# Differential-attention core of a hybrid trunk: both score rows reduced and awaited in one step, squares of the head outputs on GpSimd a tile at a time, one more item in flight

## The chip, the cores and the metric

The kernel runs on one core of one Trainium2 chip. The metric is the device time of one execution in microseconds (us). The core has TensorE (PE, with its weight loads PEld), the Vector engine (DVE), the Scalar engine (ACT), GpSimd (POOL) and the DMA queues issued by SyncE (SP). Matrix products land in PSUM, here eight banks of 512 float32 per partition; everything else lies in SBUF.

## The reference, cut to what matters

The trunk has two layers: a convolution and state-space mixer with a dense SwiGLU, then differential attention with a mixture of experts. The change is inside the attention of the second layer: 512 tokens, 8 pairs of heads, head size 64, values of 128 per pair.

```
q, k = apply_rope(rmsnorm(q, q_norm)), apply_rope(rmsnorm(k, k_norm))
lam = exp(sum(lam_q1*lam_k1)) - exp(sum(lam_q2*lam_k2)) + lambda_init
for q0 in range(0, s, 128):                       # 4 query blocks
    sc = q[q0:q0+128] @ k[:q0+128].T / sqrt(64)   # 16 heads = 8 pairs x 2
    p  = softmax(where(kpos//64 <= qpos//64, sc, -inf))
    a  = p[first of pair] - lam * p[second of pair]
    o  = a @ v[:q0+128]                           # 128 x 128 for each pair
o = rmsnorm(o, sub_norm) * (1 - lambda_init)      # mean square over the 128 of a pair
out = o @ w_o
```

## The kernel before, in words

Everything is float32. The attention core (lines 702 to 735 on TensorE, 952 to 984 on the Scalar engine, 1395 to 1428 on the Vector engine) works through 32 items. An item is one query tile `i` of 128 tokens and one pair; `items` (line 702) goes through the tiles from last to first, so items 0 to 7 see w = 512 keys, 8 to 15 see 384, 16 to 23 see 256, and 24 to 31 see 128. Each engine runs the same Python loop over `n` with its own program order; semaphores tie them together. The word "step n" below means iteration n of that loop.

In step n of the kernel before:

- TensorE computes the two score rows of item n (line 713, with the 64-column mask as a second small product, line 715) into banks 0 and 1 or 2 and 3, turns the difference of item n-2 (line 724, four 128x128 transposes at w = 512) into bank 4 or 5, and multiplies the turned difference of item n-3 with v (line 733) into bank 6 or 7, in this order.
- The Vector engine takes the maximum of each score row of item n in an instruction of its own (line 1402), drains, multiplies both by -SCALE (line 1404, `bias_ready`), then for item n-1 takes the reciprocals of the two softmax sums (line 1412), forms -lambda * sum0 / sum1 (line 1414) and the difference `probs0 + s * probs1` (line 1418), and last scales the output of item n-3 from PSUM into `o_tok` (line 1423, `heads_evac`).
- The Scalar engine takes the two exponentials of item n with their sums (line 962), with a drain and a semaphore after each (line 964), copies the turned difference of item n-2 to SBUF (line 971, `diffT_ready`), and squares the output of item n-3 with a sum into `head_ss` (line 976). In step 31 it takes the square root over the sums of the first three tiles (line 980).
- GpSimd does nothing in the core. In the rest of the layer it makes the low parts `w_lo` of the weights (line 1022); its next one follows the core.

`probs`, `diff`, `diffT` and the score banks have two buffers each, `soft` (maxima, sums, factors) four. After the loop the Vector engine scales the four tiles of `o_tok` by the reciprocal roots (`heads_norm`, lines 1381 to 1393), and TensorE turns them and begins the output projection (line 524). The Vector engine's program order in a step is thus maxima(n), difference(n-1), output(n-3).

Of the kernel before, what the change touches and what calls it, by code (L numbers as in the profile page):

```python
# [16 lines left out]
F32 = mybir.dt.float32  # L17
# [7 lines left out]
P = 128  # L25
# [16 lines left out]
NEG = -1e30  # L42
# [54 lines left out]
def build_trunk(nc, t, y_dram, h_slots):  # L97
# [74 lines left out]
    probs, o = place("probs", [P, 2, 2, SEQ], F32, scratch)  # L172
    diff, o = place("diff", [P, 2, SEQ], F32, o)
    diffT, o = place("diffT", [P, 2, SEQ], F32, o)
    soft, _ = place("soft", [P, 4, 8], F32, scratch + 65536)
# [17 lines left out]
    def sem(name):  # L193
# [31 lines left out]
    diff_turned, diffT_ready, heads_out, heads_evac = (sem("diff_turned"), sem("diffT_ready"),  # L225
                                                       sem("heads_out"), sem("heads_evac"))
# [138 lines left out]
    def _(pe):  # L365
# [338 lines left out]
        for n in range(N + 3):  # L704
            if n < N:
                pair, i = items[n]
                w = P * (i + 1)
                if n >= 2:
                    pe.wait_ge(exp_done, 2 * (n - 1))
                for m in range(2):  # L710
                    r = slice(64 * m, 64 * m + 64)
                    b = 2 * (n % 2) + m
                    pe.matmul(ps[:, b, 0:w], qT[r, pair, i * P:(i + 1) * P], kT[r, pair, 0:w],
                              start=True, stop=False, skip_group_check=True)
                    mm = pe.matmul(ps[:, b, w - 64:w], att_small[r, 0:P], att_small[r, P:P + 64],
                                   start=False, stop=True, skip_group_check=True)
                mm.then_inc(scores_done, 1)
            if 2 <= n < N + 2:
                pair, i = items[n - 2]
                pe.wait_ge(diff_ready, n - 1)  # L720
                if n >= 4:
                    pe.wait_ge(diffT_ready, n - 3)
                for b in range(i + 1):
                    mm = pe.transpose(ps[:, 4 + n % 2, b * P:(b + 1) * P],
                                      diff[:, n % 2, b * P:(b + 1) * P], ident[:])
                mm.then_inc(diff_turned, 1)
            if n >= 3:
                pair, i = items[n - 3]
                pe.wait_ge(diffT_ready, n - 2)
                if n >= 5:  # L730
                    pe.wait_ge(heads_evac, n - 4)
                for b in range(i + 1):
                    mm = pe.matmul(ps[:, 6 + (n - 3) % 2, 0:P], diffT[:, (n - 3) % 2, b * P:(b + 1) * P],
# [14 lines left out]
    def _(act):  # L748
# [205 lines left out]
        for n in range(N + 3):  # L954
            if n < N:
# [3 lines left out]
                if n >= 2:  # L959
                    act.wait_ge(diff_ready, n - 1)  # L960
                for m in range(2):
                    act.activation(probs[:, n % 2, m, 0:w], ps[:, 2 * (n % 2) + m, 0:w], ACT.Exp, scale=SCALE,
                                   bias=soft[:, n % 4, m:m + 1], accum_out=soft[:, n % 4, 2 + m:3 + m])
                    act.drain().then_inc(exp_done, 1)
            if 2 <= n < N + 2:
                pair, i = items[n - 2]
                w = P * (i + 1)
                act.wait_ge(diff_turned, n - 1)
                if n >= 4:
                    act.wait_ge(heads_out, n - 3)  # L970
                act.activation(diffT[:, n % 2, 0:w], ps[:, 4 + n % 2, 0:w], ACT.Copy).then_inc(diffT_ready, 1)
            if n >= 3:
                pair, i = items[n - 3]
                act.wait_ge(heads_evac, n - 2)
# [4 lines left out]

# [34 lines left out]
    def _(pool):  # L1014
# [70 lines left out]
        for half in range(2):  # L1085
# [7 lines left out]
            low_parts(u0 + FF_HALF - 1 + AHEAD)  # L1093
        low_parts(N_UNITS - 1)
# [3 lines left out]
    def _(dve):  # L1098
# [220 lines left out]
        dve.wait_ge(att_in, 128)  # L1319
        for i in range(2):  # L1320
# [21 lines left out]
        for r in (0, 64):  # L1342
            dve.memset(att_small[r:r + 1, 0:64], NEG)
# [51 lines left out]
        for n in range(N + 3):  # L1395
            if n < N:
                pair, i = items[n]
                w = P * (i + 1)
                s2 = soft[:, n % 4, :]
                dve.wait_ge(scores_done, n + 1)  # L1400
                for m in range(2):
                    dve.reduce_max(s2[:, 6 + m:7 + m], ps[:, 2 * (n % 2) + m, 0:w], AX.X)
                dve.drain()
                dve.tensor_scalar(s2[:, 0:2], s2[:, 6:8], -SCALE, None, ALU.mult).then_inc(bias_ready, 1)
            if 1 <= n <= N:

                pair, i = items[n - 1]
                w = P * (i + 1)
                b = (n - 1) % 2
                s2 = soft[:, (n - 1) % 4, :]  # L1410
                dve.wait_ge(exp_done, 2 * n)
                dve.reciprocal(s2[:, 4:6], s2[:, 2:4])
                dve.drain()
                dve.tensor_scalar(s2[:, 5:6], s2[:, 5:6], s2[:, 2:3], stat[:, 61:62], ALU.mult, ALU.mult)
                if n >= 3:
                    dve.wait_ge(diff_turned, n - 2)
                dve.drain()
                dve.scalar_tensor_tensor(diff[:, b, 0:w], probs[:, b, 1, 0:w], s2[:, 5:6], probs[:, b, 0, 0:w],
                                         ALU.mult, ALU.add).then_inc(diff_ready, 1)
            if n >= 3:  # L1420
                pair, i = items[n - 3]
                dve.wait_ge(heads_out, n - 2)
                dve.tensor_scalar(o_tok[:, i, pair * P:(pair + 1) * P], ps[:, 6 + (n - 3) % 2, 0:P],
                                  soft[:, (n - 3) % 4, 4:5], None, ALU.mult).then_inc(heads_evac, 1)
            if n > N:
                heads_norm(n - N - 1)
        heads_norm(NT - 2)
# [914 lines left out]
```

## Time and profile before

| | |
|---|---|
| time, median of 3 runs (lowest, highest) | 2041.79 us (2039.48, 2042.93) |
| time of the profiled execution | 2043.4 us |
| span of the profiled execution | 2041.6 us |
| PE busy | 1971.8 us (97%) |
| DVE busy | 749.8 us (37%) |
| ACT busy | 652.1 us (32%) |
| POOL busy | 490.9 us (24%) |
| mean granted TensorE clock | 0.983 |

The span runs from the first instruction to the last; the execution's own time lies 1.8 us above it. The shares are means over stages with different limits. The attention core runs from the first score product at 920.2 us to the first product of the output projection at 1011.9 us, 4.5% of the span.

### The profile page before, as it was taken

The numbers are of one execution on the slowest core, as the hardware profiler recorded it, in microseconds if no ns is written. First come the engines' busy times: TensorE is split into PE (matmuls) and PEld (weight loads), VectorE is DVE, ScalarE is ACT, GpSimd is POOL, SyncE is SP. The second block draws the span as 40 slices with busy tenths as digits, with TensorE's granted clock in tenths as the row PEclk, the third lists the DMA queues.
The fourth block names the chain that finished last, engine by engine and source line by source line (L and its number), as shares of the span: only waits on it lengthen the run. The fifth ranks groups of instructions, "written<-read, shape, count | busy, mean of one in ns | idle before, by whom it ended". The sixth has DMA issues, their size and how long they took to land.

```text
span 2041.6 us, 28889 instructions
## 1 busy us (share of the span) xinstructions
PE 1971.8 (97%) x11899; PEld 1731.5 (85%) x11899; DVE 749.8 (37%) x1138; ACT 652.1 (32%) x1061; POOL 490.9 (24%) x246
## 2 busy tenths in 40 slices
PE   7999999999999999998899999999999999999996
PEld 6787778888888888886688999999999999888885
DVE  4625564210010005948722000010010101989896
ACT  4333223232222224337630000000000011878784
POOL 3446664265445544540011000000000000000010
PEclk9999999999999999999898999999999999999998
DMA  7862222243233232330007977888888898999995
GB/s 241 298 197 74 63 73 93 73 124 93 92 95 103 88 105 75 101 104 1 22 1 268 322 241 260 300 299 302 276 305 288 284 312 278 377 372 374 361 396 212
DMA packets 295087, 405.38 MB, mean 199 GB/s; under 512 B 11264, under 2 KB 211018, under 8 KB 294954
## 3 DMA queue, kind: packets, MB, share of 16 engines
q1 hardware_dynamic: 292650, 395.11, 57.4%
q0 software_dynamic: 2304, 8.39, 1.1%
q8 instruction: 96, 1.57, 0.3%
q14 instruction: 37, 0.30, 0.0%
HBM read 372.67 MB, written 30.80 MB: 198 GB/s over the span
## 4 chain that ended last, share of the span: by engine, by line
PE 88%; DVE 3%; ACT 2%; DVEq 2%; POOL 2%; issue 1%; DMA 1%; SPq 0%; POOLq 0%; ACTq 0%
PE ps L1729 20%; PE ps L1736 10%; PE ps L375 5%; PE ps L376 5%; PE ps L377 5%; PE ps L393 5%; PE ps L394 5%; PE ps L395 5%; PE ps L1787 4%; PE ps L1789 4%; PE ps L1788 4%; PE ps L410 2%; PE ps L412 2%; PE ps L411 2%; DVEq L1186 1%
## 5 line engine op out<-in xcount | busy, mean ns | idle before, releaser
L1022 POOL TENSOR_TENSOR w_lo<-raw,w_hi 128x1024 fp32r<-128x1024 f32 (+1 forms) x159 | 390.3, 2463 | 462.7 <-ACT w_hi L758 462.7
L1563 DVE TENSOR_TENSOR s_lo<-s_raw,s_hi 128x1024 fp32r<-128x1024 f32 x198 | 236.9, 1222 | 28.1 <-ACT s_hi L1933 22.6
L2183 DVE TENSOR_TENSOR hid<-ps,silu_g 128x160 f32<-128x160 f32 x110 | 35.7, 324 | 550.1 <-ACT silu_g L1908 550.1
L1729 PE MATMUL ps<-xT,w_gate 128*128 128x132 f32 (+1 forms) x1760 | 226.6, 282 | 4.6 <-issue 4.0
L758 ACT ACTIVATE w_hi<-raw 128x1024 fp32r<-128x1024 f32 (+1 forms) x159 | 164.8, 1043 | 205.1 <-PE ps L395 136.4
L375 PE MATMUL ps<-act_a_hi,w_hi 128*128 128x512 f32 x568 | 226.3, 398 | 0.0
L1729 PE MATMUL ps<-xT,w_up 128*128 128x132 f32 (+1 forms) x1760 | 224.4, 281 | 0.0
L1908 ACT ACTIVATE silu_g<-ps 128x160 f32<-128x160 f32 x110 | 33.5, 304 | 593.3 <-PE ps L1729 593.3
L1933 ACT ACTIVATE s_hi<-s_raw 128x1024 fp32r<-128x1024 f32 x198 | 206.7, 1061 | 51.0 <-PE ps L1789 46.5
L377 PE MATMUL ps<-act_a_hi,w_lo 128*128 128x512 f32 x568 | 221.2, 389 | 0.0
L376 PE MATMUL ps<-act_a_lo,w_hi 128*128 128x512 f32 x568 | 221.1, 389 | 0.0
L1729 PEld LDWEIGHTS ps<-xT,w_gate 128*128 128x128 f32 x1760 | 216.2, 191 | 5.1 <-issue 4.2
L1736 PE MATMUL ps<-hid,w_down 128*128 128x132 f32 (+1 forms) x1760 | 214.8, 281 | 0.0
L1729 PEld LDWEIGHTS ps<-xT,w_up 128*128 128x128 f32 x1760 | 214.6, 190 | 0.0
L1736 PEld LDWEIGHTS ps<-hid,w_down 128*128 128x128 f32 x1760 | 209.8, 190 | 0.2
L2028 POOL DMA_INDIRECT y_lower<-y_rows,idx x4 | 5.3, 1334 | 825.8 <-DMA y_rows<-y_rows_sb 824.8
L375 PEld LDWEIGHTS ps<-act_a_hi,w_hi 128*128 128x128 f32 x568 | 106.7, 188 | 27.1 <-issue 5.3
L376 PEld LDWEIGHTS ps<-act_a_lo,w_hi 128*128 128x128 f32 x568 | 106.7, 188 | 24.6 <-issue 2.9
L377 PEld LDWEIGHTS ps<-act_a_hi,w_lo 128*128 128x128 f32 x568 | 106.6, 188 | 22.3
L1787 PE MATMUL ps<-s_hi,s_x_hi 128*128 128x512 f32 (+1 forms) x288 | 109.8, 381 | 0.0
L1789 PE MATMUL ps<-s_hi,s_x_lo 128*128 128x512 f32 (+1 forms) x288 | 107.9, 375 | 0.0
L1788 PE MATMUL ps<-s_lo,s_x_hi 128*128 128x512 f32 (+1 forms) x288 | 107.0, 372 | 0.0
(355 smaller groups left out, 2949.1 us busy)
## 6 DMA issues: line engine op xcount, KB each, us to landing
w_gate<-in_moe_w_gate SPq DMA_DIRECT2D x55, 1024.0 KB, 5.6
w_up<-in_moe_w_up SPq DMA_DIRECT2D x55, 1024.0 KB, 8.5
w_down<-in_moe_w_down SPq DMA_DIRECT2D x55, 1024.0 KB, 11.0
s_raw<-in_moe_w_gate SPq DMA_DIRECT2D x33, 1024.0 KB, 7.6
s_raw<-in_moe_w_up SPq DMA_DIRECT2D x33, 1024.0 KB, 8.3
s_raw<-in_moe_w_down SPq DMA_DIRECT2D x33, 1024.0 KB, 7.7
raw<-in_even_w_in SPq DMA_DIRECT2D x43, 512.0 KB, 4.5
raw<-in_attn_w_qkv SPq DMA_DIRECT2D x24, 512.0 KB, 3.8
```

The lines of the kernel that those rows point to most:

```text
L375: pe.matmul(ps[:, bank, :], wh, xh[:, k, :], start=(k == 0), stop=False)
L376: pe.matmul(ps[:, bank, :], wh, xl[:, k, :], start=False, stop=False)
L377: last = pe.matmul(ps[:, bank, :], wl, xh[:, k, :], start=False, stop=(k == KD - 1))
L758: act.activation(w_hi[:, u % HL_SLOTS, 0:size(u)], raw[:, u % RAW_SLOTS, 0:size(u)], ACT.Copy).then_inc(hi_done, 1)
L1022: pool.tensor_tensor(w_lo[:, u % HL_SLOTS, 0:size(u)], raw[:, u % RAW_SLOTS, 0:size(u)], flat(w_hi[:, u % HL_SLOTS, 0:size(u)]), ALU.subtr ...
L1563: return eng.tensor_tensor(s_lo[u % S_HL][:], s_raw[u // 2 % S_RAW][:, u % 2, :], s_hi[u % S_HL][:].bitcast(F32), ALU.subtract)
L1729: mm = pe.matmul(ps[:, bank, i * CAP:i * CAP + width], w_slots[s][i][:, k, c:c + P], xT[:, k, 0:width], start=(k == 0), stop=(k == KD - 1))
L1736: mm = pe.matmul(ps[:, d // 3, (d % 3) * CAP:(d % 3) * CAP + width], w_slots[s][2][:, f % 2, d * P:(d + 1) * P], hid[:, f, 0:width], start ...
L1787: pe.matmul(out, sh, wh, start=first, stop=False, skip_group_check=True)
L1788: pe.matmul(out, sh, wl, start=False, stop=False, skip_group_check=True)
L1789: return pe.matmul(out, sl, wh, start=False, stop=last, skip_group_check=True)
L1933: act.activation(s_hi[u % S_HL][:], s_raw[q % S_RAW][:, u % 2, :], ACT.Copy).then_inc(s_high, 1)
```

## The change

The gain of the q norm is multiplied by -SCALE once, before the loop, so that the scores in PSUM are already the negated scaled ones; the mask adds +1e30. One `tensor_reduce` with min over both banks gives the two biases directly. The exponential uses scale -1, and one drain and one semaphore follow both. `probs` gets a third buffer, `soft` eight. Transposes run on item n-3 and head products on item n-4. The Vector engine's order in a step becomes minima(n), output(n-4), difference(n-1), and the factor is made by one `scalar_tensor_tensor`. The squares of the first three tiles are taken on GpSimd, each tile in two instructions of 128x512 once its eight outputs are in `o_tok`, and summed on the Vector engine by a reduction of 128x1024 at the end of steps 15, 23 and 31; the Scalar engine squares only the last tile's items. The Scalar engine's root in step 31 waits for the three sums.

```diff
--- before.py
+++ after.py
@@ -39,7 +39,7 @@
-NEG = -1e30
+MASKED = 1e30
@@ -169,10 +169,10 @@
     sq_tmp, o = place("sq_tmp", [P, SEQ], F32, o)
     qT, o = place("qT", [P, KD, SEQ], F32, SEQ * NT * 4 * 2)
     kT, o = place("kT", [P, KD, SEQ], F32, o)
-    probs, o = place("probs", [P, 2, 2, SEQ], F32, scratch)
+    probs, o = place("probs", [P, 3, 2, SEQ], F32, scratch)
     diff, o = place("diff", [P, 2, SEQ], F32, o)
-    diffT, o = place("diffT", [P, 2, SEQ], F32, o)
-    soft, _ = place("soft", [P, 4, 8], F32, scratch + 65536)
+    diffT, o = place("diffT", [P, 2, SEQ], F32, scratch + 3 * NT * D * 4)
+    soft, _ = place("soft", [P, 8, 8], F32, scratch + 65536)
     o_tok, o = place("o_tok", [P, NT, D], F32, scratch + NT * D * 4)
 
     h_tok, _ = place("h_tok", [P, NT, D], F32, NT * D * 4)
...
@@ -701,12 +702,12 @@
 
         items = [(pair, i) for i in reversed(range(NT)) for pair in range(PAIRS)]
         N = len(items)
-        for n in range(N + 3):
+        for n in range(N + 4):
             if n < N:
                 pair, i = items[n]
                 w = P * (i + 1)
                 if n >= 2:
-                    pe.wait_ge(exp_done, 2 * (n - 1))
+                    pe.wait_ge(exp_done, n - 1)
                 for m in range(2):
                     r = slice(64 * m, 64 * m + 64)
                     b = 2 * (n % 2) + m
@@ -715,22 +716,22 @@
                     mm = pe.matmul(ps[:, b, w - 64:w], att_small[r, 0:P], att_small[r, P:P + 64],
                                    start=False, stop=True, skip_group_check=True)
                 mm.then_inc(scores_done, 1)
-            if 2 <= n < N + 2:
-                pair, i = items[n - 2]
-                pe.wait_ge(diff_ready, n - 1)
-                if n >= 4:
-                    pe.wait_ge(diffT_ready, n - 3)
+            if 3 <= n < N + 3:
+                pair, i = items[n - 3]
+                pe.wait_ge(diff_ready, n - 2)
+                if n >= 5:
+                    pe.wait_ge(diffT_ready[(n - 5) % 2], (n - 5) // 2 + 1)
                 for b in range(i + 1):
-                    mm = pe.transpose(ps[:, 4 + n % 2, b * P:(b + 1) * P],
-                                      diff[:, n % 2, b * P:(b + 1) * P], ident[:])
+                    mm = pe.transpose(ps[:, 4 + (n - 3) % 2, b * P:(b + 1) * P],
+                                      diff[:, (n - 3) % 2, b * P:(b + 1) * P], ident[:])
                 mm.then_inc(diff_turned, 1)
-            if n >= 3:
-                pair, i = items[n - 3]
-                pe.wait_ge(diffT_ready, n - 2)
-                if n >= 5:
-                    pe.wait_ge(heads_evac, n - 4)
+            if n >= 4:
+                pair, i = items[n - 4]
+                pe.wait_ge(diffT_ready[(n - 4) % 2], (n - 4) // 2 + 1)
+                if n >= 6:
+                    pe.wait_ge(heads_evac, n - 5)
                 for b in range(i + 1):
-                    mm = pe.matmul(ps[:, 6 + (n - 3) % 2, 0:P], diffT[:, (n - 3) % 2, b * P:(b + 1) * P],
+                    mm = pe.matmul(ps[:, 6 + (n - 4) % 2, 0:P], diffT[:, (n - 4) % 2, b * P:(b + 1) * P],
                                    v_tok[:, b, pair * P:(pair + 1) * P], start=(b == 0), stop=(b == i))
                 mm.then_inc(heads_out, 1)
         first_tokens(4, U_WO, heads_tile, act_b_hi, act_b_lo)
@@ -951,32 +952,33 @@
             act.activation((qT, kT)[n // 8][:, n % 8, :], ps[:, n % 4, :], ACT.Copy).then_inc(qk_evac[0], 1)
         items = [(pair, i) for i in reversed(range(NT)) for pair in range(PAIRS)]
         N = len(items)
-        for n in range(N + 3):
+        for n in range(N + 5):
             if n < N:
                 pair, i = items[n]
                 w = P * (i + 1)
                 act.wait_ge(bias_ready, n + 1)
-                if n >= 2:
-                    act.wait_ge(diff_ready, n - 1)
+                if n >= 3:
+                    act.wait_ge(diff_ready, n - 2)
                 for m in range(2):
-                    act.activation(probs[:, n % 2, m, 0:w], ps[:, 2 * (n % 2) + m, 0:w], ACT.Exp, scale=SCALE,
-                                   bias=soft[:, n % 4, m:m + 1], accum_out=soft[:, n % 4, 2 + m:3 + m])
-                    act.drain().then_inc(exp_done, 1)
-            if 2 <= n < N + 2:
-                pair, i = items[n - 2]
+                    act.activation(probs[:, n % 3, m, 0:w], ps[:, 2 * (n % 2) + m, 0:w], ACT.Exp, scale=-1.0,
+                                   bias=soft[:, n % 8, m:m + 1], accum_out=soft[:, n % 8, 2 + m:3 + m])
+                act.drain().then_inc(exp_done, 1)
+            if 3 <= n < N + 3:
+                pair, i = items[n - 3]
                 w = P * (i + 1)
-                act.wait_ge(diff_turned, n - 1)
-                if n >= 4:
-                    act.wait_ge(heads_out, n - 3)
-                act.activation(diffT[:, n % 2, 0:w], ps[:, 4 + n % 2, 0:w], ACT.Copy).then_inc(diffT_ready, 1)
-            if n >= 3:
-                pair, i = items[n - 3]
-                act.wait_ge(heads_evac, n - 2)
+                b = (n - 3) % 2
+                act.wait_ge(diff_turned, n - 2)
+                if n >= 5:
+                    act.wait_ge(heads_out, n - 4)
+                act.activation(diffT[:, b, 0:w], ps[:, 4 + b, 0:w], ACT.Copy).then_inc(diffT_ready[b], 1)
+            if n >= N - PAIRS + 5:
+                pair, i = items[n - 5]
+                act.wait_ge(heads_evac, n - 4)
                 act.drain()
                 act.activation(sq_tmp[:, 0:P], o_tok[:, i, pair * P:(pair + 1) * P], ACT.Square,
                                accum_out=head_ss[:, 8 * i + pair:8 * i + pair + 1])
             if n == N - 1:
-
+                act.wait_ge(o_sum, NT - 1)
                 act.activation(head_ss[:, 40:64], head_ss[:, 8:32], ACT.Sqrt, scale=1.0 / P,
                                bias=stat[:, 60:61]).then_inc(o_rms, 1)
         act.drain()
@@ -1091,6 +1093,22 @@
                 pool.tensor_tensor(ff_lo[:, f, :], ff_val[:, n % 2, :], flat(ff_hi[:, f, :]),
                                    ALU.subtract).then_inc(ff_lo_done, 1)
             low_parts(u0 + FF_HALF - 1 + AHEAD)
+        low_parts(U_WO + AHEAD - 1)
+
+        items = [(pair, i) for i in reversed(range(NT)) for pair in range(PAIRS)]
+        N = len(items)
+
+        def square_half(k, h):
+            tt, c = NT - 1 - k, slice(512 * h, 512 * h + 512)
+            pool.wait_ge(heads_evac, PAIRS * (k + 1))
+            pool.tensor_tensor(htmp[:, c], o_tok[:, tt, c], o_tok[:, tt, c], ALU.mult).then_inc(o_sq, 1)
+
+        for n in range(N):
+            k, at = (n - 12) // PAIRS, (n - 12) % PAIRS
+            if 0 <= k < NT - 1 and at < 2:
+                if at == 0 and k:
+                    pool.wait_ge(o_sum, k)
+                square_half(k, at)
         low_parts(N_UNITS - 1)
 
 
@@ -1317,6 +1335,9 @@
                 add_to_x(G_DOWN[0] + 1, u0 + FF_HALF - 1, 512)
         add_and_norm(2, G_DOWN[1] + 1, U_QKV - 1)
         dve.wait_ge(att_in, 128)
+
+        dve.tensor_scalar(att_small[:, 0:HD], att_small[:, 0:HD], -SCALE, None, ALU.mult)
+        dve.drain()
         for i in range(2):
             g1, g2 = att_small[:, HD * i:HD * i + 32], att_small[:, HD * i + 32:HD * i + 64]
             b1, b2 = (g.unsqueeze(1).to_broadcast([P, NT, 32]) for g in (g1, g2))
@@ -1340,7 +1361,7 @@
-            dve.memset(att_small[r:r + 1, 0:64], NEG)
+            dve.memset(att_small[r:r + 1, 0:64], MASKED)
@@ -1392,39 +1413,40 @@
             if j >= 2:
                 turned_low(4, j - 2, act_b_hi, act_b_lo, small[:, 63:64])
 
-        for n in range(N + 3):
+        for n in range(N + 4):
             if n < N:
                 pair, i = items[n]
                 w = P * (i + 1)
-                s2 = soft[:, n % 4, :]
                 dve.wait_ge(scores_done, n + 1)
-                for m in range(2):
-                    dve.reduce_max(s2[:, 6 + m:7 + m], ps[:, 2 * (n % 2) + m, 0:w], AX.X)
-                dve.drain()
-                dve.tensor_scalar(s2[:, 0:2], s2[:, 6:8], -SCALE, None, ALU.mult).then_inc(bias_ready, 1)
+                dve.tensor_reduce(soft[:, n % 8, 0:2], ps[:, 2 * (n % 2):2 * (n % 2) + 2, 0:w], AX.X, ALU.min
+                                  ).then_inc(bias_ready, 1)
+            if n >= 4:
+                pair, i = items[n - 4]
+                dve.wait_ge(heads_out, n - 3)
+                dve.tensor_scalar(o_tok[:, i, pair * P:(pair + 1) * P], ps[:, 6 + (n - 4) % 2, 0:P],
+                                  soft[:, (n - 4) % 8, 4:5], None, ALU.mult).then_inc(heads_evac, 1)
             if 1 <= n <= N:
 
-                pair, i = items[n - 1]
-                w = P * (i + 1)
-                b = (n - 1) % 2
-                s2 = soft[:, (n - 1) % 4, :]
-                dve.wait_ge(exp_done, 2 * n)
+                s2 = soft[:, (n - 1) % 8, :]
+                dve.wait_ge(exp_done, n)
                 dve.reciprocal(s2[:, 4:6], s2[:, 2:4])
                 dve.drain()
-                dve.tensor_scalar(s2[:, 5:6], s2[:, 5:6], s2[:, 2:3], stat[:, 61:62], ALU.mult, ALU.mult)
+                dve.scalar_tensor_tensor(s2[:, 6:7], s2[:, 5:6], stat[:, 61:62], s2[:, 2:3], ALU.mult, ALU.mult)
                 if n >= 3:
                     dve.wait_ge(diff_turned, n - 2)
                 dve.drain()
-                dve.scalar_tensor_tensor(diff[:, b, 0:w], probs[:, b, 1, 0:w], s2[:, 5:6], probs[:, b, 0, 0:w],
-                                         ALU.mult, ALU.add).then_inc(diff_ready, 1)
-            if n >= 3:
-                pair, i = items[n - 3]
-                dve.wait_ge(heads_out, n - 2)
-                dve.tensor_scalar(o_tok[:, i, pair * P:(pair + 1) * P], ps[:, 6 + (n - 3) % 2, 0:P],
-                                  soft[:, (n - 3) % 4, 4:5], None, ALU.mult).then_inc(heads_evac, 1)
+                pair, i = items[n - 1]
+                w = P * (i + 1)
+                dve.scalar_tensor_tensor(diff[:, (n - 1) % 2, 0:w], probs[:, (n - 1) % 3, 1, 0:w], s2[:, 6:7],
+                                         probs[:, (n - 1) % 3, 0, 0:w], ALU.mult, ALU.add).then_inc(diff_ready, 1)
+            if n in (15, 23, 31):
+                k = n // PAIRS - 1
+                i = NT - 1 - k
+                dve.wait_ge(o_sq, 2 * (k + 1))
+                dve.reduce_sum(head_ss[:, 8 * i:8 * i + 8], htmp[:].rearrange("p (h d) -> p h d", h=8), AX.X
+                               ).then_inc(o_sum, 1)
             if n > N:
                 heads_norm(n - N - 1)
-        heads_norm(NT - 2)
         heads_norm(NT - 1)
         for j in (NT - 2, NT - 1):
             turned_low(4, j, act_b_hi, act_b_lo, small[:, 63:64])
```

## Rows read from the trace of the kernel before

**Rows 1.** Stretch, length, busy PE PEld DVE ACT POOL, clock, DMA, GB/s
```profile
920.00:1003.00 83.00, 70.39 (x490) 50.88 (x490) 68.86 (x222) 63.01 (x214) 0.00 (x0) 0.95 0.01 1
```

**Rows 2.** Chain of waits, one cycle at 512 keys: start us, us, what
```profile
936.18 0.69 DVE soft L1402
936.87 0.60 DVEq L1403
937.75 0.69 ACT probs L962
938.62 0.69 ACT probs L962
939.56 0.61 ACT diffT L971
940.21 1.16 PE ps L733 x8
...
942.66 0.69 DVE soft L1402
```

**Rows 3.** Groups by form, 920 to 1012 us: busy us, mean ns, idle
```profile
L1402 DVE TENSOR_REDUCE soft<-ps 128x1 f32<-128x512 f32 x16 | 10.3, 684 | 3.0 <-PE ps L715 3.0
...
L1418 DVE SCALAR_TENSOR_TENSOR diff<-probs,soft 128x512 f32<-128x512 f32 x8 | 6.0, 752 | 0.6
...
L1418 DVE SCALAR_TENSOR_TENSOR diff<-probs,soft 128x128 f32<-128x128 f32 x8 | 2.8, 352 | 0.6
```

**Rows 4.** Timeline, Vector engine, one item at 512 keys: start us, us
```profile
934.13 0.16 DVE L1412 RECIPROCAL soft<-soft 128x2 f32<-128x2 f32 x1
...
934.72 0.75 DVE L1418 SCALAR_TENSOR_TENSOR diff<-probs,soft 128x512 f32<-128x512 f32 x1
...
935.39 0.34 DVE L1423 TENSOR_SCALAR o_tok<-ps,soft 128x128 f32<-128x128 f32 x1
```

**Rows 5.** Timeline, one item at 128 keys, Scalar engine, TensorE
```profile
995.41 0.19 ACT L976 ACTIVATION_READ_ACCUMULATOR sq_tmp<-o_tok 128x1 f32 x1
...
995.50 0.35 ACT L962 ACTIVATE probs<-ps,soft 128x128 f32<-128x128 f32 x1
...
996.66 0.28 ACT L971 ACTIVATE diffT<-ps 128x128 f32<-128x128 f32 x1 [0.16 <-PE ps L724]
...
996.99 0.49 PE L733 MATMUL ps<-v_tok,diffT 128*128 128x128 f32 x2 [0.48 <-ACT diffT L971]
```

**Rows 6.** GpSimd, Vector: by line (ns min/median/max), timeline, by form (mean ns)
```profile
L1366 DVE TENSOR_TENSOR q_tok<-rot_sum,head_ss x8: 691/2613/2619, 808.8 to 844.3; 128x512 f32<-128x512 f32 x8
...
811.66 2.93 POOL L1022 TENSOR_TENSOR w_lo<-raw,w_hi 128x1024 fp32r<-128x1024 f32 x1 [3.93 <-ACT w_hi L758]
...
L1091 POOL TENSOR_TENSOR ff_lo<-ff_val,ff_hi x22: 1289/1295/1301, 431.3 to 716.3; 128x512 fp32r<-128x512 f32 x22
...
293.83 4.26 DVE L1235 TENSOR_TENSOR mix<-mix,cbm 128x512 f32<-128x512 f32 x2
...
L1196 DVE SCALAR_TENSOR_TENSOR dts<-dts 128x64 f32<-128x64 f32 x1 | 0.5, 527 | 0.1
```

**Rows 7.** Chain of waits, from the first exponential to the output projection
```profile
923.12 0.69 ACT probs L962
...
1001.49 0.37 ACT probs L962
...
1003.43 1.28 ACT L980
...
1006.73 1.22 DVE o_tok L1390
1007.95 0.26 DVE o_tok L1423
...
1011.86 0.50 PE ps L524
```

**Rows 8.** As rows 1, for 927 to 929 us
```profile
927.00:929.00 2.00, 2.00 (x6) 0.86 (x6) 1.76 (x5) 1.12 (x3) 0.00 (x0) 0.50 0.04 8
```

More of the change, by code:

```diff
@@ L224, in build_trunk @@
                                                      sem("exp_done"), sem("diff_ready"))
-    diff_turned, diffT_ready, heads_out, heads_evac = (sem("diff_turned"), sem("diffT_ready"),
-                                                       sem("heads_out"), sem("heads_evac"))
+    diff_turned, heads_out, heads_evac = sem("diff_turned"), sem("heads_out"), sem("heads_evac")
+    diffT_ready = (sem("diffT_even"), sem("diffT_odd"))
+    o_sq, o_sum = sem("o_sq"), sem("o_sum")
     o_rms = sem("o_rms")
```

## The prediction, written before the changed kernel was run

> **What bounds the kernel now.** The page first: TensorE is busy for 97% of the span, but that is the mean over long matmul stages that the change does not touch. So I read the stretch of the attention core by itself. There TensorE is busy 70.4 us of 83, the Vector engine 68.9 and the Scalar engine 63.0, GpSimd not at all [rows 1]. No engine is full; a loop of waits through all three should be looked for, and the chain of waits shows it [rows 2]. Its seven pieces repeat: the maxima (0.69 and 0.60), a small step that makes the biases (the exponential starts 1.57 us after the first maximum), two exponentials (0.88 us apart, 1.81 to the copy), the copy of a turned difference (0.65 to the next start), then the head product (1.16) and the scores of the next item but one (2.45 from 940.21 to the next maximum at 942.66). That is 6.48 us for two items, 3.24 for one. Each engine fills some 3.0 of these 3.24. The loop takes two items because the copy stands behind the exponential in the Scalar engine's order and the scores behind the head product in TensorE's. The core gets shorter only if this loop does, or if its replacement is shorter.
>
> **The bias and the exponentials.** One reduction of 1024 elements replaces two of 512. By the slope of the difference (752 - 352) / 384 = 1.04 ns an element, it takes 0.684 + 512 x 0.00104 = 1.22 us [rows 3]; the small step and a drain go. The exponential starts 1.25 us after the reduction instead of 1.57: 0.32 gained. Bounds: if a reduction over two banks costs as two, 1.37, gain 0.17. The drain between the exponentials goes. An accumulator read that no drain follows lets the next exponential start 0.09 us after its own start [rows 5]; the second exponential now starts 0.88 - 0.68 = 0.20 us earlier. Bounds 0 and 0.20; I take 0.20, as the row is the same pair of operations. The old loop would be 6.48 - 0.32 - 0.20 = 5.96, and TensorE's own order (head product 1.16, scores, transposes) needs about 3.00 an item, so 6.0 would be the floor for two.
>
> **The order on the Vector engine, a new loop.** The output copy now stands ahead of the difference. Output(n-4) waits for the head product of TensorE's step n, and behind it on the Vector engine are queued the reciprocals, the factor, difference(n-1) and the reduction of item n+1, whose exponential in turn stands ahead of the copy that the head product of step n+2 needs. This closes a loop of two steps: head product 1.16 and 0.06 to be seen; output copy 0.26 to the next start [rows 7]; reciprocal to difference 0.59, difference to the next start 0.67 [rows 4]; reduction to exponential 1.25; exponential to copy 1.81 - 0.20 = 1.61; copy to product 0.65 [rows 2]. Sum 6.25 us, 3.13 an item. At 128 keys: product 0.49, seen 0.06, output 0.26, factor 0.59, difference 0.27, reduction 0.15 + 0.27 + 0.03 = 0.45, exponential to copy 1.16 - 0.20 = 0.96, rounded to 0.95, copy to product 0.33: 3.40, 1.70 an item [rows 3 to 5]. The one-element factor I take at its old cost; a tenth less or more is 0.1 in each double step. The pieces grow evenly with width between those ends. In the loop before, the output copy came last and this path was shorter than the loop of rows 2, since the reduction did not wait for it through the difference.
>
> **The squares.** Taking them off the Scalar engine gives it back about 0.48 us an item, but it is not in either loop behind the copy; I count nothing for it, and what hides it is that the Scalar engine waits for the bias anyway. What comes in their place is counted: six GpSimd instructions of 128x512, 1.30 us each [rows 6], and three reductions of 128x1024 on the Vector engine, 1.22 less an overlap of 0.07 = 1.15 each. The reductions at steps 15 and 23 stand between a difference and the next reduction, inside the new loop: 2.3 us. The one at step 31 counts in the tail.
> GpSimd starts its first half when the eighth output of a tile is written, so at steps 11, 19 and 27, and just then the Vector engine issues factor and difference. Vector instructions with both inputs in SBUF take 0.69 us alone and 2.61 in most cases while the low parts run on GpSimd [rows 6]; an instruction of 64 elements took 0.53. Where several GpSimd instructions stood in a row, two Vector ones took 4.26 together [rows 6]. So the factor (two SBUF inputs now) waits for the first half, and the difference, issued after a drain, for the second. Without it the difference starts 0.26 + 0.59 = 0.85 us after the output copy; with it 0.43 + 2 x 1.30 = 3.0. That is 2.1 us for each tile, 6.3 for three. Bounds: nothing if the pairs never meet, which the semaphore at that very place makes unlikely, and 2.6 x 3 = 7.8. I take 6.3. Loops without slack pass such a delay on whole; all five disturbances (at 11, 15, 19, 23, 27) fall on the same one of the two interleaved loops, so they add up to 8.6.
> The Trainium skill ("SBUF — State Buffer", section "Who interferes with whom") says that a Vector instruction with two SBUF inputs and a GpSimd instruction that reads SBUF exclude each other for the whole instruction, the one that starts first winning, whatever the shapes. By that rule the one-element factor is held as well, and the sum is 6.3; if a small operand passed freely, only the difference would be held, by the first half, and it would be 3 x 1.0. The 0.53 us of a 64-element instruction [rows 6] speaks for the rule; one of a single element is not in the trace.
>
> **Fill and tail.** The first exponential starts 0.32 us earlier than 923.12 [rows 7]. During the first four items no head product exists that anything waits for, so the items come by scores, reduction and exponential alone, also without the halved clock that TensorE had after its early wait [rows 8]. I follow them with the same pieces: exponentials 0, 2, 4, 6 at 922.8, 926.9, 931.9, 938.8. From there twelve double steps to item 30 (6.0 at first, as widths mix, 3.40 at the end) sum to 56.3: 995.1, and item 31 at 996.8. Before, it was at 1001.49 [rows 7]. So without the disturbances the loop gains 4.6; with the 8.6 it is 4.0 late.
> In the tail the projection came 10.37 us after exponential 31 (1011.86 - 1001.49). Now the Scalar engine's root waits for the third sum, which stands behind difference(30): about 2.7 us after exponential 31; the table load of 1.28 and the root follow, then the copy of item 29, its product, and three more outputs, with norms of 1.22 between them [rows 7]: I get 11.5, a loss of 1.1 us.
> The q gain's multiplication adds a small instruction where the Vector engine waits for the first squares of q: nothing, or 0.3 if that cover were gone. Memory moves and the extra buffers cost no instruction.
>
> **Sum.** -4.6 + 8.6 + 1.1 = +5.1 us. The execution profiled took 2043.4 (span 2041.6), so 2048.5; against the median of the runs, which lies 1.6 lower, 2041.8 + 5.1 = 2046.9. What can be told from no change is 0.2%, 4.1 us, that is 2037.7 to 2045.9.
>
> **Rivals.**
> A, the forecast: new loop, and both factor and difference held. +5.1, 2046.9. For it: the orders, and rows 6. Against: it needs the timing at step 11 to be as written. 0.38.
> B, the same but held only once a tile (a one-element factor passes, or starts first): 3 x 1.1 less, +1.8, 2043.6. 0.27.
> C, the new loop does not bind: head products come early enough, through the extra item in flight, and the floor is TensorE's 3.00 (at 128 keys 2.88 for two). The mean saving is 0.38 in each of twelve double steps, 4.6; holds once a tile, and slack takes 0.3 from each of five disturbances, 1.5: +1.8 - 4.6 - 1.5 = -4.3, 2037.5, faster. For it: the Vector engine has 0.3 us to spare an item. Against: the loop is only 0.25 us above the floor at 512 keys but 0.5 at 128, and I see nothing that would cut it. 0.18.
> D, the clock: TensorE was granted 0.50 at 927 to 929 us [rows 8], after it had waited for the first exponential. Five delays of 1 to 2 us, each a wait of TensorE, might bring this back each time; a product of 1.16 then takes 2.3 and the loop grows by some 1.5 us for such a stretch. Two or three of them: +3.5 on top of A, 2050.4, slower. 0.17.
>
> **How the numbers follow.** A's own spread (bounds 0.17 against 0.32 for the reduction, the factor) is about 2.5 us to either side; six tenths of it lie above 2045.9, the rest within. Slower: 0.23 + 0.17 = 0.40, with a little of B 0.42. Same: 0.15 + 0.25 = 0.39 with the near end of C. Faster: C, 0.19. The range takes C's near end and D's: 2037.5 to 2050.5.
>
> **What would show it.** The reduction of 128x2x512 near 1.22 us, the bias step gone; the second exponential 0.68 us after the first at 512 keys. In the chain, output copy, factor and difference between head product and reduction (if instead scores lead to the reduction throughout, C). One factor or difference of over 1 us at items 7, 15 and 23, the factor of one element among them (B, if only one instruction is long). The sums at 1.2 us with the reduction of the next item right behind. The table load later after exponential 31 than the 1.94 us of before. The clock in windows behind steps 11 and 19. I am wrong if the core, 920.2 to 1011.9 before, is shorter than 88 us or longer than 101.

## The result, and the profile after

| | before | after |
|---|---|---|
| time, median of 13 runs (lowest, highest) | 2041.76 us (2038.36, 2044.44) | 2046.79 us (2044.24, 2047.59) |
| ratio to before, 95% interval | | 1.0021 [1.0014, 1.0029] |
| span of the profiled execution | 2041.6 us | 2044.7 us |
| core: first score product to first product of the output projection | 91.65 us | 95.32 us |

The change makes the kernel slower, by 5.0 us in the medians (4.3 by the ratio, its interval 2.9 to 5.9) and by 3.7 us in the core of the two profiled executions. From here on "core" is that stretch. It is read from one trace of each kernel, and it is sharper than the medians, because the 1950 us around it vary by a few microseconds (1946.2 to 1954.0 us over ten traces here). No trace was repeated for one kernel, so the core's own scatter is not known; experiment 5 shows 0.3 us that its edit does not explain.

The new loop stands in the changed kernel's chain of waits at 512 keys (start us, us, what). Lines 734, 1426, 1440, 1421, 963 and 973 are 733, 1423, 1418, 1402, 962 and 971 of before. The first head product is released by a copy of the Scalar engine, the last closes the loop; pieces of up to 0.22 us are left out:

```profile
930.99 1.17 PE ps L734 x8
932.18 0.35 DVE o_tok L1426
932.98 0.75 DVE diff L1440
933.73 1.15 DVE soft L1421
934.90 0.69 ACT probs L963
935.67 0.67 ACT probs L963 x2
936.50 0.61 ACT diffT L973
937.15 1.16 PE ps L734 x8
```

In [rows 2] the maximum followed the scores; here it follows the output copy and the difference. The cycle is 937.15 - 930.99 = 6.16 us where it was 6.48. The parts that should become cheaper did. In the groups by form (mean ns behind the busy time) the minimum over 2x512 takes 1220 ns against two of 684 in [rows 3]:

```profile
L1421 DVE TENSOR_REDUCE soft<-ps 128x2 f32<-128x1024 f32 x8 | 9.7, 1220 | 1.7 <-PE ps L716 1.6
...
L1446 DVE TENSOR_REDUCE head_ss<-htmp 128x8 f32<-128x1024 f32 x3 | 3.6, 1213 | 0.0
```

On the Scalar engine's timeline (start us, us) the two exponentials of an item start 0.67 us apart, 0.87 before [rows 2]:

```profile
922.00 0.69 ACT L963 ACTIVATE probs<-ps,soft 128x512 f32<-128x512 f32 x1 [3.23 <-DVE soft L1421]
...
922.67 0.68 ACT L963 ACTIVATE probs<-ps,soft 128x512 f32<-128x512 f32 x1
```

What eats the gain is at steps 11, 19 and 27. The timeline of the Vector engine and GpSimd at step 11 (start us, us, engine, line, operation):

```profile
952.58 0.35 DVE L1426 TENSOR_SCALAR o_tok<-ps,soft 128x128 f32<-128x128 f32 x1
...
953.01 2.04 POOL L1104 TENSOR_TENSOR htmp<-o_tok 128x512 f32<-128x512 f32 x2 [43.38 <-DVE o_tok L1426]
...
953.08 0.99 DVE L1434 SCALAR_TENSOR_TENSOR soft<-soft,stat 128x1 f32<-128x1 f32 x1
...
954.14 1.32 DVE L1440 SCALAR_TENSOR_TENSOR diff<-probs,soft 128x384 f32<-128x384 f32 x1
...
955.38 0.95 DVE L1421 TENSOR_REDUCE soft<-ps 128x2 f32<-128x768 f32 x1
```

The squares start 0.07 us ahead of the one-element factor here, and within 0.01 us of it at steps 19 and 27. The factor takes 0.99 us instead of 0.22 and the difference 1.32 instead of 0.62, the one held by the first half, the other by the second. From output copy to next minimum it is 955.38 - 952.58 = 2.80 us, and 1.32 in the step before (950.19 to 951.51): a hold of 1.48, and in the same way 1.54 at each of steps 19 and 27, 4.6 together. Behind the second hold TensorE's granted clock falls to its lower level, 0.50, from about 979 to 986 us (stretch, length, busy us of PE, PEld, DVE, ACT, POOL, granted clock):

```profile
920.00:1003.00 83.00, 67.73 (x482) 51.38 (x478) 64.72 (x149) 48.28 (x154) 6.11 (x6) 0.92 0.00 1
978.00:982.00 4.00, 2.25 (x10) 1.70 (x11) 2.64 (x9) 2.81 (x10) 0.00 (x0) 0.69 0.00 0
982.00:986.00 4.00, 4.00 (x22) 3.30 (x21) 2.57 (x7) 1.40 (x5) 0.00 (x0) 0.50 0.01 2
```

Over the same 83 us as [rows 1] TensorE is busy for 67.7 us instead of 70.4, at 0.92 instead of 0.95. The Scalar engine, freed of 24 squares, is busy for 48.3 instead of 63.0; experiments 2 and 7 show that this time is worth nothing here.

### The profile page after: what moved, and what is told of

It is laid out like the page before. It is cut to its first block, busy times and chain, and to the rows that moved or that the text cites. A ratio compares the mean times of both kernels' runs of the same rounds, so it can differ in the third digit from the quotient of the medians.

```text
span 2044.7 us, 28701 instructions
## 1 busy us (share of the span) xinstructions
PE 1969.6 (96%) x11899; PEld 1732.3 (85%) x11899; DVE 750.5 (37%) x1078; ACT 639.7 (31%) x1013; POOL 497.6 (24%) x252
## 4 chain that ended last, share of the span: by engine, by line
PE 88%; DVE 4%; ACT 2%; POOL 2%; DVEq 2%; issue 1%; DMA 1%; POOLq 0%; SPq 0%; ACTq 0%
PE ps L1751 20%; PE ps L1758 10%; PE ps L376 5%; PE ps L377 5%; PE ps L378 5%; PE ps L394 5%; PE ps L396 5%; PE ps L395 5%; PE ps L1809 4%; PE ps L1811 4%; PE ps L1810 4%; PE ps L411 2%; PE ps L412 2%; PE ps L413 2%; DVEq L1204 1%
```

## Experiments

In each, "exponential k" is the time from exponential 0 to exponential k in the trace. Before: 31 at 78.37; after: 12 at 34.36, 20 at 56.40, 24 at 67.64, 31 at 81.88.

**1. Output copy back behind the difference** (the moved lines in words).

```diff
-            if n >= 4:  (output copy of item n-4, between minima and factor)
+            if n >= 4:  (the same lines, behind the difference of item n-1)
```

> The changed kernel with the output copy put back behind the difference in the Vector engine's step. 'Core' is the time from the first score product to the first product of the output projection: 91.7 us before, 95.3 after. Theory (the output copy ahead of the difference closes a loop of 6.2 us for two items): the core loses some 4.6 us of loop, the holds by GpSimd shrink from 1.5 to about 0.8 us since the squares now start beside the reduction, and the stretch at half clock goes: core 87 to 89 us, time 6 to 8 us under the changed kernel. Rival (the extra item in flight has made the order harmless, only the holds count): core 93 us or more, time at most 2 us less.

Core 86.41 us, time 2037.26, ratio 0.9971 [0.9961, 0.9982] to before. The core is 0.6 us better than my bound, and the medians differ from the changed kernel by 9.5 us where I had 6 to 8. The chain at 512 keys, from head product to head product, is that of before with the cheaper parts, 937.46 - 931.49 = 5.97 us (5.96 forecast as the old loop):

```profile
931.49 1.16 PE ps L734 x8
932.65 1.07 PE ps L714 x4
933.72 0.20 PE ps L716 x4
...
933.94 1.24 DVE soft L1421
...
935.20 0.69 ACT probs L963
...
936.81 0.61 ACT diffT L973
...
937.46 1.16 PE ps L734 x8
```

This run alone mixes the loop with smaller holds: the longest factor is 0.95 us, and of the three differences behind the squares only the last is still held (1.05 us). The next ones part them.

**2. Squares back on the Scalar engine, order kept.**

```diff
-            if n >= N - PAIRS + 5:
+            if n >= 5:
-                act.wait_ge(o_sum, NT - 1)
-   (GpSimd's squares and the Vector engine's sums)
```

> The changed kernel with the squares of every item on the Scalar engine as before, no GpSimd work and no sums in the core, everything else kept. Theory: this takes away the holds (3 x 1.47), two sums inside the loop (2 x 1.13) and the stretch at half clock (about 1.6): core 87 to 89 us against 95.3, and the Scalar engine, which gets 0.48 us an item back to do, is the bound at 128 keys only and by less than 0.1 an item. Rival (the Scalar engine was what the squares had to leave): core 93 us or more.

Core 86.93 us, just under my 87 to 89, time 2038.37, ratio 0.9977 [0.9967, 0.9987]. Exponential 31 at 73.50: the rest of the change, new order and all, gains 4.9 us in the loop. The move to GpSimd costs 8.4 of core. The rival falls: the Scalar engine had room.

**3. Squares a little later.**

```diff
             pool.wait_ge(heads_evac, PAIRS * (k + 1))
+            pool.wait_ge(diff_ready, PAIRS * k + 11 + h)
```

> The changed kernel with each GpSimd half also waiting for a difference to be done (first half for that of its own step, second half for that of the next step), so that neither factor nor difference meets it. Theory: the three holds of 1.47 go and with them part of the half clock: core 89.5 to 91.5 us, time 4 to 6 us under the changed kernel, all factors 0.22 us. Rival (other waits cover the holds): core within 1 us of 95.3.

Core 89.44, time 2040.78, ratio 0.9988 [0.9979, 0.9997]. The longest factor is 0.46 us, so not all are at the 0.22 I had expected; no difference is held. Exponential 12 is at 32.89 (1.47 earlier than in the changed kernel), 20 at 53.41 (2.99), 24 at 62.82 (4.82), 31 at 76.00 (5.88). So the holds are 1.5 us each and pass on whole, and between 20 and 24, where nothing is held and both kernels take one sum, another 1.8 goes. What differs there in the two traces is the clock: 0.50 from 980 to 984 us in the changed kernel, and 1.00 throughout in this run, where these exponentials are at 975.15 and 984.56. I put the 1.8 down to it; no run changes the clock alone.

**4. Is it a busy GpSimd or one that reads SBUF?** Memsets of like length at the same place; the squares of three tiles are left out.

```diff
-            pool.tensor_tensor(htmp[:, c], o_tok[:, tt, c], o_tok[:, tt, c], ALU.mult).then_inc(o_sq, 1)
+            first half:  pool.memset(htmp[:], 1.0).then_inc(o_sq, 1)
+            second half: pool.memset(rot_tmp[:], 1.0); pool.memset(rot_sum[:], 1.0).then_inc(o_sq, 1)
```

> The changed kernel with the GpSimd squares replaced by memsets of about the same length (one of 1024, then two of 512 elements), at the same place and behind the same waits; the squares of three tiles are left out. Theory (the holds come from both engines reading SBUF): factor and difference at 0.22 and 0.35 to 0.62 us throughout, core 89 to 91 us. Rival (a busy GpSimd, or its semaphores, holds the Vector engine): factors of about 1 us at steps 11, 19 and 27, core 94 us or more. The core alone is read, since the routing behind it works on other numbers.

Core 89.50 (time 2399.6 in its one run, not compared: behind the core it works on other numbers), exponentials 12, 20, 24 and 31 at 32.89, 53.39, 62.79 and 76.06: the kernel of experiment 3 within 0.06 us. Timeline of GpSimd at step 11 (start us, us):

```profile
952.80 0.95 POOL L1108 MEMSET htmp<- 128x1024 f32 x1 [43.35 <-DVE o_tok L1430]
953.69 0.52 POOL L1105 MEMSET rot_tmp<- 128x512 f32 x1
954.16 0.52 POOL L1106 MEMSET rot_sum<- 128x512 f32 x1
```

And all 32 factors, by line (ns min/median/max):

```profile
L1438 DVE SCALAR_TENSOR_TENSOR soft<-soft,stat x32: 219/220/221, 923.6 to 1000.7; 128x1 f32<-128x1 f32 x32
```

GpSimd is busy for nearly as long as with the squares (1.9 us against 2.04) and no factor takes more than 221 ns; the longest difference is 0.75 us, as without a hold. A memset writes SBUF and reads nothing, so it is the reading that holds the Vector engine. The Trainium skill ("SBUF — State Buffer", section "Who interferes with whom") has the same: a Vector instruction takes its second SBUF input through the read interface that it shares with GpSimd, so it contends with a GpSimd instruction that reads SBUF and not with one that only writes. The traces agree, and in the changed kernel one element was enough, 0.99 for 0.22 us.

**5. Cheap sums.** The sums take the first column of each head alone; the rest is left out.

```diff
-   htmp[:].rearrange("p (h d) -> p h d", h=8), AX.X
+   htmp[:].rearrange("p (h d) -> p h d", h=8)[:, :, 0:1], AX.X
```

> The changed kernel with its three sums cut to the first column of each head (the rest of the sum is left out). Theory: each sum costs about 0.2 instead of 1.21 us; two stand in the loop and one holds back the table load: 2 to 3 us of the core (92.3 to 93.3 us). Rival (the Vector engine waits for the head product anyway, so a sum is free): core within 0.7 us of 95.3.

Core 92.05, 3.3 us less and 0.25 beyond my bound, with sums of 159 ns instead of 1213. Exponential 31 comes 3.26 earlier and the tail (exponential 31 to the projection) is the same to 0.01 us (10.83 and 10.84), so the third sum, in the tail, is free. Not all of the 3.26 is sums: 0.32 of it is there at exponential 12 (34.04 here), before the first sum. From 924 to 928 us this run was granted the full clock and the changed kernel was not (stretch as above, the changed kernel first):

```profile
924.00:928.00 4.00, 3.76 (x19) 2.21 (x16) 3.49 (x6) 2.44 (x8) 0.00 (x0) 0.61 0.02 4
924.00:928.00 4.00, 3.05 (x22) 1.78 (x20) 3.78 (x6) 2.33 (x8) 0.00 (x0) 1.00 0.01 4
```

At exponential 20 the gain is 1.37 (55.03 here), so the first sum cost 1.05. Between exponentials 20 and 24 it grows to 3.58 (64.06 here), 1.2 more than one sum of 1.05: there the changed kernel was granted 0.94, 0.50 and 0.71 in the four microseconds each from 976, 980 and 984 us, this run 0.84, 0.73 and 1.00. Its time as a whole (2226.33) says nothing, since the sums change which tokens go to which expert.

**6. Both mends at once.** Output copy last and squares on the Scalar engine (the edits of 1 and 2).

> Both together: output copy behind the difference, and all squares on the Scalar engine, nothing on GpSimd, no sums. Against the kernel that has only the squares moved back (core 86.9 us) it differs in the order alone. Theory (the order costs 0.2 to 0.5 us in each double step where TensorE or the Scalar engine is not the bound): core 84 to 85.5 us. Rival (with the holds gone the order is harmless): core 86.5 to 87.5 us.

Core 82.97, time 2033.96, ratio 0.9960 [0.9947, 0.9974]. Against experiment 2 the order alone is worth 3.96 us of core, with no GpSimd in it: more than the 1.4 to 2.9 I had expected. Exponential 31 is at 69.55 against 73.50, and exponential 12 at 31.73 against 32.81, so three quarters of it come behind exponential 12. Exponentials 8, 16 and 24 come 0.62, 1.75 and 3.27 us earlier: most of it falls at 384 and 256 keys, and only 0.68 behind exponential 24, at 128 keys, where by my sum the order should cost most over TensorE's own floor. Why it does not is open.

**7. Output last, squares on GpSimd, second half one output later.**

```diff
-            pool.wait_ge(heads_evac, PAIRS * (k + 1))
+            pool.wait_ge(heads_evac, PAIRS * (k + 1) + h)
```

> Output copy behind the difference, squares on GpSimd, the second half of a tile one output later than the first, so that each half runs beside the minimum of the next item. Against the kernel with the order alone changed (core 86.4 us, factors held up to 0.95 us) only the holds should differ. Theory: factors at 0.22 us, 0.5 to 0.7 us less at each of three tiles, of which slack had taken a part: core 84.8 to 86.4 us. Rival (the sums and slack decide): core 86.4 us unchanged.

Core 83.54, time 2035.33, ratio 0.9967 [0.9955, 0.9979]; 1.3 us beyond my bound. The longest factor is 0.66 us, not 0.22. With the order mended and the holds nearly gone GpSimd is no better a place for the squares than the Scalar engine: the intervals of this run and experiment 6 overlap, and its core is 0.6 us longer.

**8. One item less in flight, order as changed.**

```diff
-            if 3 <= n < N + 3:  transposes and copy of items[n - 3]
-            if n >= 4:          head product and output of items[n - 4]
+            if 2 <= n < N + 2:  items[n - 2]
+            if n >= 3:          items[n - 3]
```

> The changed kernel with transposes on item n-2, head products and outputs on item n-3, as before; everything else as changed. Theory (the loop has the same pieces whatever item the copy turns, so an extra item in flight buys fill and pays drain): core within 1.5 us of 95.3, same time. Rival (the extra item in flight is what pays for the new order): core 98 us or more.

Core 100.30, time 2050.42, ratio 1.0042 [1.0028, 1.0055]. My theory fell, the rival holds. The chain shows what I had overlooked, a loop of one step (the last gap, 0.05 us, is left out):

```profile
934.79 0.66 PE ps L725 x4
935.44 0.91 PE ps L734 x8
936.38 0.35 DVE o_tok L1426
...
936.87 0.22 DVE soft L1434
937.16 0.76 DVE diff L1440
937.97 0.66 PE ps L725 x4
```

Difference(n-1), its transposes in TensorE's next step, the head product behind them in program order, the output copy that waits for it, and the next difference behind that: 937.97 - 934.79 = 3.18 us an item, without minimum or exponential. With one more item in flight the transposes are of an older item and this loop is two steps long, so it does not bind.

**9. Only the first part, on the kernel before.** Negated scores, one minimum, one drain and one semaphore; order, depth and squares as before. The minimum's part of the edit:

```diff
-                for m in range(2):
-                    dve.reduce_max(s2[:, 6 + m:7 + m], ps[:, 2 * (n % 2) + m, 0:w], AX.X)
-                dve.drain()
-                dve.tensor_scalar(s2[:, 0:2], s2[:, 6:8], -SCALE, None, ALU.mult).then_inc(bias_ready, 1)
+                dve.tensor_reduce(soft[:, n % 4, 0:2], ps[:, 2 * (n % 2):2 * (n % 2) + 2, 0:w], AX.X, ALU.min
+                                  ).then_inc(bias_ready, 1)
```

> The kernel before with only the bias and exponential part of the change: negated scores, one minimum over both rows, one drain and one semaphore after both exponentials. Order on the Vector engine, items in flight and squares stay as before. Theory (this part is the whole gain; the loop is 5.96 instead of 6.48 us at 512 keys, and an extra item is of use only to the order with the output copy ahead): core within 1.5 us of the 83.0 us of the kernel with output last and squares on the Scalar engine, time 6.5 to 9 us under the kernel before. Rival (the extra item in flight gives something of its own in any order): core 85.5 us or more.

Core 82.81, time 2034.04, ratio 0.9955 [0.9941, 0.9969]: as good as experiment 6 with its deeper buffers, with a much smaller edit. These two are the best versions found, 8 us under before and some 13 under the change. Its chain runs along TensorE for long stretches (start us, us):

```profile
932.65 1.12 PE ps L733 x8
933.77 1.06 PE ps L713 x4
934.84 0.17 PE ps L715 x4
935.01 0.58 PE ps L724 x4
935.59 0.04 issue
935.63 1.16 PE ps L733 x8
```

That is head product, scores, transposes and the next head product with 0.04 us between: 2.98 us an item, which is TensorE's own work for it.

**10. Only the order, on the kernel before.** The output copy (line 1423 with its wait) moved ahead of the reciprocals.

> The kernel before with only the output copy moved ahead of the difference, one item less in flight than the changed kernel. Theory, as mended by the run with one item less: two loops, one of two steps (6.48 + 0.29 = 6.77 us at 512 keys) and one of a single step (transposes, product, output copy, factor, difference, 3.2 us at 512, some 2.1 at 128 keys where 1.83 was the step): core 93.5 to 96.5 us against 91.7, time 2 to 5 us over the kernel before. Rival (the order costs only where the minimum is merged): core 91.7 us.

Core 98.48, time 2048.83, ratio 1.0030 [1.0018, 1.0042]. The core is worse than I said by 2 us and the medians differ from before by 7.1, not 2 to 5; the loop of one step binds at all widths, and takes 3.36 us at 512 keys (transposes at 932.52, 935.87, 939.25, 942.61 in its chain), not 3.2: the old factor of 0.27 us and two small gaps are in it, and the product, issued late, shows 1.01 to 1.05.

## Why the prediction was right, and where its parts were not

Forecast +5.1 us, measured +5.0 in the medians; in the traces the core grew by 3.7. The mechanism was the one forecast, case A, but the sizes of the holds, the clock and the tail in it were off.

- The bias and exponential: right. 1.22 us forecast and 1.220 measured for the minimum, 0.20 forecast and 0.20 measured for the second exponential. Experiment 9 adds what I had not asked: this part alone is a gain of 8.8 us in the core.
- The new loop: right in place, 6.25 us forecast and 6.16 measured at 512 keys. Without the disturbances I had exponential 31 at 74.0 after exponential 0 (996.8 - 922.8); experiment 2, which has none, shows 73.50. The half microsecond is in the fill (exponential 6 at 16.0 forecast, 15.52 there); the twelve double steps to exponential 30 were forecast at 56.3 and take 56.37.
- The holds: both factor and difference were held, as said, but a square takes GpSimd 1.04 us (two halves 2.04), not the 1.30 of the low parts of [rows 6]. With 1.04 the forecast's own formula gives 0.43 + 2.08 - 0.85 = 1.66 for a hold; 1.48 to 1.54 were measured, not 2.1. That is 4.6 us for three, where the sum had 6.3. This is the term that was mis-sized most. That row was the wrong neighbour: it subtracts and writes fp32r. The products in float32 that GpSimd makes earlier in the kernel before take 2.15 and 1.90 us for 128x1024 (lines 1051 and 1047), close to two squares. Which property of the row costs the time no run parts.
- The sums: 2.3 forecast. Experiment 5 gives 1.05 for the first, so 2.1 for the two, and 3.3 in all with the clock at two places in it.
- The clock: I had it at nothing in the sum and at 3.5 in rival D. It came at 978 to 986 us, behind the hold of step 19, and exponential 24 comes 1.8 us later than in experiment 3 beyond the holds; by exponential 31 1.3 of it is left (5.88 less 4.6 of holds), experiment 3 having a shorter stretch of its own (0.57 from 986 to 990 us). D was half right: the loss came once, and D had it two or three times. The clock is also at 0.50 from 1000 to 1004 us, behind the third hold, but there it is in the kernel before as well.
- The tail: forecast +1.1 by a wait for the third sum, measured +0.47. The table load that the root needs does not wait. In the timeline of both engines (start us, us) it starts at 1005.62, 1.74 us after exponential 31 (1.94 before), while the sum runs until 1006.51, and the root starts right behind the load:

```profile
1005.30 1.21 DVE L1446 TENSOR_REDUCE head_ss<-htmp 128x8 f32<-128x1024 f32 x1
...
1005.62 1.28 ACT L982 ACT_TABLE_LOAD   x1
...
1006.91 0.31 ACT L982 ACTIVATE head_ss<-head_ss,stat 128x24 f32<-128x24 f32 x1
```

- What the tail lost is not settled. With the output last and the squares on the Scalar engine, the kernel with the extra item and its buffers has a tail of 10.81 (experiment 6) against 10.14 (experiment 9); but in the changed kernel itself one item less saves only 0.15 (10.69 in experiment 8 against 10.84).
- The sum from the traces: -0.31 for the first exponential; 73.50 - 78.37 = -4.87 for the loop; 76.00 - 73.50 = +2.50 from experiment 2 to 3, which holds the two sums and experiment 3's own stretch of low clock; 81.88 - 76.00 = +5.88 from there to the changed kernel, 4.6 of it holds and 1.3 clock; +0.47 tail. Together 3.67, as it must be, since each term starts where the last one ends; only the names of the parts are argued. The ratio's interval, 2.9 to 5.9, holds both 3.7 and 5.0; I can't divide the rest. That the forecast met the median to 0.1 us is luck: its holds were 1.7 too large, its tail 0.6 too large, its gain by the loop 0.6 too small and its clock 1.3 too small.
- Small slips in it: 996.8 - 1001.49 is -4.7, not -4.6, and 3.0 - 0.85 is 2.15 a tile, 6.45 for three, not 6.3. It had each engine filling some 3.0 of 3.24 us an item. From 932 to 944 us the trace of before has TensorE busy for 10.97, the Vector engine for 10.36 and the Scalar engine for 9.55 of 12 us, that is 2.96, 2.80 and 2.58 an item, so the Scalar engine had the most room.
- The rivals: B (one hold a tile) fell by the 1.32 us difference. C (the loop does not bind) fell by the chain of the changed kernel and by experiments 1 and 6.
- What the prediction missed: it gave the extra item no part in the new order. It is what makes that order bearable, since without it the loop has one step and the core is 5.0 us longer (experiment 8).

Open: why the halved clock came behind step 19 and not behind 11 or 15, whose hold and sum are of like length. The traces show only that TensorE was busy for less before it: 1.78 us of the four from 976 to 980 us, against 2.57 from 956 to 960 and 2.63 from 968 to 972, where the clock stayed at 1.00.

## What to carry to other kernels

Follow every loop of waits through all engines, with its number of steps, before moving an instruction within one engine's order: an instruction that waits, placed ahead of work that others need, holds that work back even where its engine has idle time, and the number of items in flight decides whether the loop that this closes is one step long or two (6.8 us of core by the order alone in experiment 10, 4.0 with one more item in flight in experiments 2 and 6). Work moved to an idle GpSimd is not free if it reads SBUF while the Vector engine works on two SBUF inputs (1.5 us for each pair of squares here). Put its start behind the last such instruction, and look whether the engine that it relieves was waiting anyway. Try the parts of a bundled change one at a time: here one was worth -8 us in the medians and the others took 13 back.

## What the runs showed of the hardware that was not expected

- A GpSimd product of a tile with itself, 128x512 in float32, takes 1.04 us; a subtraction of two tiles of that size into fp32r takes 1.30 [rows 6].
- A one-element Vector instruction with two SBUF inputs waits for a GpSimd product like a large one (0.99 to 1.05 us for 0.22), and a memset does not hold it at all (221 ns at most). Two such products in a row held two Vector instructions in a row, one each.
- The Scalar engine's next table was loaded while the sum that the root waits for still ran (load from 1005.62, sum until 1006.51), so the load's 1.28 us hid the wait. The trace does not show whether the load stands ahead of the wait in the engine's program.
